# A chunked two-direction recurrence with stacked operands: products of 128 rows, transposes, and a new order of work

## What is computed

```python
def step(S, inp):
    rt, wt, kt, vt, at, bt = inp
    sa = jnp.einsum('bhvk,bhk->bhv', S, at)
    S = S * wt[:, :, None, :] + sa[..., None] * bt[:, :, None, :] + vt[..., None] * kt[:, :, None, :]
    return S, jnp.einsum('bhvk,bhk->bhv', S, rt)
...
s_fin, yd = wkv_scan(rh, decay, kd, vh, -kk, kk * a, S0[d], reverse=(d == 1))
```

## Time and profile before

| what | value |
|---|---|
| median of 3 runs | 2350.64 us (2346.11 to 2356.69) |
| the profiled execution's own time | 2349.85 us |
| its span | 2348.2 us |
| scan of layer 0, first product to last read | 415.1 to 621.3 us |
| scan of layer 1, window that holds it | 1617 to 1820 us |
| granted clock of PE, mean | 0.954 |

### The profile page before, as it was taken

How to read it: one execution, slowest core, us unless ns; L and a number is a source line. 1 busy time by engine, 2 the same in 40 slices (tenths; PEclk the granted TensorE clock), 3 DMA queues, 4 the chain that set the end, 5 groups by cost and what they waited for, 6 DMA issues and landing times. The chain is left out here.

```text
span 2348.2 us, 53901 instructions
## 1 busy us (share of the span) xinstructions
PE 2101.7 (90%) x23898; PEld 1349.7 (57%) x23898; DVE 720.6 (31%) x1768; ACT 487.9 (21%) x1120; POOL 274.7 (12%) x463
## 2 busy tenths in 40 slices
PE   6999899899899999999999789898999899987784
PEld 2454443889644444446556465554898788754442
DVE  1033334777431011310100032546676311200002
ACT  2123312333220000301111132323332301110011
POOL 0000000443100001101111100001343000011111
PEclk8999999899999999999999989998899999998996
DMA  7148716000121212448999821110000344799993
GB/s 287 61 154 344 305 65 226 3 4 4 56 90 54 108 54 108 181 161 328 398 383 395 306 90 51 69 50 1 4 4 4 146 159 188 274 378 397 395 406 122
DMA packets 55828, 399.91 MB, mean 170 GB/s; under 512 B 6672, under 2 KB 22928, under 8 KB 33648
## 3 DMA queue, kind: packets, MB, share of 16 engines
q1 hardware_dynamic: 43440, 361.94, 39.9%
q0 software_dynamic: 8576, 23.08, 2.6%
q10 hardware_dynamic: 3648, 12.45, 1.7%
HBM read 365.47 MB, written 31.98 MB: 169 GB/s over the span
## 5 line engine op out<-in xcount | busy, mean ns | idle before, releaser
L494 PE MATMUL ps<-H,memory 128*128 128x512 f32 (+2 forms) x1728 | 615.1, 512 | 11.6 <-DMA memory<-in_w_in 9.7
L494 PEld LDWEIGHTS ps<-H,memory 128*128 128x128 f32 (+1 forms) x1728 | 327.5, 190 | 286.5 <-issue 251.6
L731 PE MATMUL ps<-memory 64*64 64x32 f32 (+2 forms) x10112 | 329.0, 229 | 33.6 <-DVE memory L1624 10.1
L994 PE MATMUL ps<-memory 128*32 128x256 f32 x5120 | 298.8, 395 | 49.2 <-DMA memory<-in_eu 47.7
L731 PEld LDWEIGHTS ps<-memory 64*64 64x64 f32 x10112 | 316.4, 142 | 43.3 <-issue 21.3
L494 PE MATMUL ps<-memory 128*128 128x512 f32 (+3 forms) x928 | 319.2, 495 | 6.2 <-issue 3.0
L994 PEld LDWEIGHTS ps<-memory 128*32 128x32 f32 x5120 | 184.8, 114 | 160.0 <-issue 71.0
L494 PEld LDWEIGHTS ps<-memory 128*128 128x128 f32 (+1 forms) x928 | 173.8, 188 | 143.6 <-issue 127.3
L1019 PE MATMUL ps<-memory 128*32 128x256 f32 x2560 | 144.8, 380 | 5.0 <-ACT memory L1342 3.8
L1914 POOL TENSOR_TENSOR memory<-memory,cons 128x256 f32<-128x256 f32 x160 | 117.9, 752 | 122.5 <-DVE memory L1596 78.7
L1019 PEld LDWEIGHTS ps<-memory 128*32 128x32 f32 x2560 | 79.6, 110 | 59.9 <-ACT memory L1342 10.1
(11 more groups left out here) (251 smaller groups left out, 1804.9 us busy)
## 6 DMA issues: line engine op xcount, KB each, us to landing
memory<-in_eg SPq DMA_DIRECT2D x32, 2048.0 KB, 17.2
memory<-in_eu SPq DMA_DIRECT2D x32, 2048.0 KB, 23.0
memory<-in_ed SPq DMA_DIRECT2D x32, 2048.0 KB, 23.4
memory<-in_w_ada SPq DMA_DIRECT2D x24, 2048.0 KB, 9.5
memory<-in_w_in SPq DMA_DIRECT2D x20, 2048.0 KB, 7.6
expert_rows<-memory SPq DMA_DIRECT2D x4, 3456.0 KB, 23.7
memory<-in_w_out SPq DMA_DIRECT2D x4, 2048.0 KB, 7.8
memory<-expert_rows ACTq DMA_DIRECT2D x19, 384.0 KB, 10.4
```

What stands on the lines that cost most here:

```text
L494: ins = mm(ps[0:M, bank, 0:w], lhs(k), rhs(k), start=(k == 0), stop=(k == n - 1))
L731: ins = mm(out[cols, j], lhs[rows, j, :], rhs[rows, j], start=(n == 0), stop=(n == len(terms) - 1))
L994: ins = mm(out_.rearrange("p (x n) -> p x n", x=2), XGT[:, k, g * GROUP:g * GROUP + GROUP], sets[b][:, 0:2, k * 512 + c * P:k * 512 + c * ...
```

## The change

- The two heads' halves are kept in tiles with j outermost, so that one weight load takes 128 columns: `bE2` and `bKk` lie side by side in `BB`. `grams` is one product of 64 rows and 128 weight columns for each head, and the two heads write to different banks (`bank`).
- U and the values of a head lie one above the other in `UV` (64 + 64 partitions); so do the masked grams (`GR`) and the turned keys (`BK`). The last two terms of `readout` and both terms of `update` become one product of 128 rows and 64 weight columns.
- `turns` and `values` use PE's transpose, one record each, of 64 rows by 128 columns, in place of products with `eye`. `pick` on ACT gathers the two directions' chunks of V.
- `correct` is split: `correct_values` behind `couple`, then `grams` of both directions, then `correct_state`, then `solve`. Nothing stands between `correct_state` and `solve`, nor between `solve` and the first join.
- `turns` of both directions stand at level 1, `readout` of both at level 2, `update` of both at level 3, all behind `join(n,0)`; levels 0 and 4 have none; `values` stands behind level 4.
- ACT takes over: the unit diagonals of `XT` (`diagonals`; DVE then writes only the pairs, by `copy_predicated`), the state's decay (`decayed_state`, four ACTIVATEs for each direction), and the first visit of each output column (`first_read`, a copy; the memset of Y on POOL goes). Signs move into `B` and the masks.

```diff
+BK = [[pairs(piece(2)) for d in range(2)] for p in range(2)]
+GR = [[pairs(piece(2)) for d in range(2)] for p in range(2)]
+UV = [pairs(piece(2)) for d in range(2)]
+BB = [pairs(piece(2)) for d in range(2)]
+GAK = pairs(piece(2))
+VC = pairs(piece(2))
 TWICE = {"XT": [[quads(inv[d][:, 512 * p:512 * p + 256]) for d in range(2)] for p in range(2)],
...
+        "L": [quads(piece(1, (3,))) for d in range(2)],
+        "bE2": [BB[d][:, :, d] for d in range(2)],
+        "bKk": [BB[d][:, :, 1 - d] for d in range(2)]}
...
+    for j, d, h in problems:
+        ins = mm(part(d, 2, p)[side(h ^ d), j], BB[d][side(h), j, d], ER[p][d][side(h), 0, j],
+                 start=True, stop=True)
...
+def values(k):
+    pe.wait_ge(sem("values_moved"), picked(l * STEPS + k))
+    for d in both:
+        pe.wait_ge(sem("joined_copied"), level(l * STEPS + k, len(LEVELS) - 1, d))
+    for j in range(RJ):
+        for h in both:
+            ins = pe.transpose(ps[:, bank(h, 3), 256 + CH * j:256 + CH * j + CH], VC[side(h), j], eye[side(h), :])
+    ins.then_inc(sem("values"), 1)
...
 def grams(k, d):
...
+    if k:
+        pe.wait_ge(sem("state"), states(l, k - 1, d))
     if k >= 2 and streams(l, k - 2):
         pe.wait_ge(sem("read"), 2 * readouts(l, k - 2) - 1 + d)
     if streams(l, k):
         pe.wait_ge(sem("queries"), 2 * readouts(l, k) - 1 + d)
...
+    for j in range(RJ):
+        for h in both:
+            ins = mm(ps[:, bank(d, h), 128 * j:128 * j + CH * wide], BB[d][side(h), j], ER[p][d][side(h), 0:wide, j],
+                     start=True, stop=True)
+    ins.then_inc(sem("grams"), 1)
...
 def turns(k, d):
     pe.wait_ge(sem("masked"), nth(l * STEPS + k, d))
...
+    for j in range(RJ):
+        for h in both:
+            ins = pe.transpose(ps[:, bank(d, h), CH * j:CH * j + CH], BB[d][side(h), j], eye[side(h), :])
+    ins.then_inc(sem("turns"), 1)
...
+def correct_values(k):
...
+    for d in both:
+        pe.wait_ge(sem("masked"), nth(N, d))
+        pe.wait_ge(sem("values_moved"), held(N, d))
+    for j, d, h in problems:
+        ins = mm(part(d, 3, 0)[side(h ^ d), j], GAK[side(1 - d), j, h], UV[d][side(1 - d), j, h],
+                 start=(j == 0), stop=False)
+    ins.then_inc(sem("values"), 1)
...
+def correct_state(k):
     N, p = l * STEPS + k, k % 2
+    pe.wait_ge(sem("values"), corrected(N))
     for d in both:
         pe.wait_ge(sem("state"), states(l, k, d))
...
+    for j, d, h in problems:
+        ins = mm(part(d, 3, 0)[side(h ^ d), j], ER[p][d][side(h), 0, j], ONCE["S"][d][side(h), j],
+                 start=False, stop=(j == RJ - 1))
+        if j == RJ - 1 and h:
+            ins.then_inc(sem("rhs"), 1)
...
 def solve(k):
     N, p = l * STEPS + k, k % 2
     for d in both:
         pe.wait_ge(sem("rhs_copied"), nth(N, d))
         pe.wait_ge(sem("inverse"), inverses(N, 5, d))
...
+    for j, d, h in problems:
+        ins = mm(part(h ^ d, 3, 1)[side(d), j], TWICE["XT"][p][d][side(h ^ d), j], ONCE["RHS"][d][side(h ^ d), j],
+                 start=True, stop=True)
+        if j == RJ - 1 and h:
+            ins.then_inc(sem("u"), 1)
...
+def readout(k):
     N, p = l * STEPS + k, k % 2
...
+    for d in both:
+        pe.wait_ge(sem("u_copied"), nth(N, d))
+        if k + 1 < STEPS:
+            pe.wait_ge(sem("masked"), nth(N + 1, d))
+        if k + 2 < STEPS:
+            pe.wait_ge(sem("turned"), carried(l, k + 1, d))
+    for j, d, h in problems:
+        mm(part(d, 1, 0)[side(h), j], ONCE["S"][d][side(h), j], ER[p][d][side(h), 1, j], start=(j == 0), stop=False)
+    for j, d, h in problems:
+        ins = mm(part(d, 1, 0)[side(h), j], UV[d][:, j, h], GR[p][d][:, j, h], start=False, stop=(j == RJ - 1))
+        if j == RJ - 1 and h:
+            ins.then_inc(sem("readout"), 1)
...
+def update(k):
...
+    for j, d, h in problems:
+        ins = mm(part(d, 0, 0)[side(h), j], BK[p][d][:, j, h], UV[d][:, j, h], start=True, stop=True)
+        if j == RJ - 1 and h:
+            ins.then_inc(sem("step"), 1)
...
 for k in range(STEPS):
     more = k + 1 < STEPS
     couple(k)
     if k:
-        correct(k - 1)
+        correct_values(k - 1)
     grams(k, 0)
+    grams(k, 1)
     if k:
+        correct_state(k - 1)
         solve(k - 1)
-    grams(k, 1)
     for n in range(len(LEVELS)):
         join(k, n, 0)
-        if n == 0 and more:
-            turns(k, 0)
-        if k and n in (1, 2) and streams(l, k - 1):
-            readout(k - 1, n - 1)
-        if k and n == 3:
-            update(k - 1, 0)
-        if n == 4 and more:
-            values(k + 1, 0)
+        if n == 1 and more:
+            for d in both:
+                turns(k, d)
+        if n == 2 and k and streams(l, k - 1):
+            readout(k - 1)
+        if n == 3 and k:
+            update(k - 1)
         join(k, n, 1)
-        if n == 0 and more:
-            turns(k, 1)
-        if k and n == 3:
-            update(k - 1, 1)
-        if n == 4 and more:
-            values(k + 1, 1)
         grow(k, n, 0)
         grow(k, n, 1)
-correct(STEPS - 1)
+    values(k)
+correct_values(STEPS - 1)
+correct_state(STEPS - 1)
 solve(STEPS - 1)
...
+quarters = lambda rows, banks, x: ps[rows, banks, 256 * x:256 * x + 256].rearrange("p b (j n) -> p b j n", n=CH)
 def turns(k, d):
     act.wait_ge(sem("turns"), carried(l, k, d))
-    act.copy(BK[k % 2][d], ps[:, 4 * d, :]).then_inc(sem("turned"), 1)
+    act.copy(by_head(BK[k % 2][d]), quarters(slice(0, P), slice(bank(d, 0), bank(d, 1) + 1), 0)).then_inc(sem("turned"), 1)
...
+def pick(k):
...
+        act.wait_ge(sem("values"), turned(l * STEPS + k - 1))
...
+    act.copy(VC, v[:, :, other:None if after < 0 else after:c - other]).then_inc(sem("values_moved"), 1)
...
 def values(k):
+    act.wait_ge(sem("values"), turned(l * STEPS + k))
...
+        rows = side(1 - d)
+        act.copy(by_head(UV[d])[rows], quarters(rows, slice(bank(0, 3), bank(1, 3) + 1), 1)).then_inc(sem("values_moved"), 1)
...
-        act.activation(flat(ONCE["RHS"][d]), part(d, 3, 0), ACT.Copy, scale=-1.0).then_inc(sem("rhs_copied"), 1)
+        act.copy(flat(ONCE["RHS"][d]), part(d, 3, 0)).then_inc(sem("rhs_copied"), 1)
...
 def solve(k):
     for d in range(2):
         act.wait_ge(sem("u"), nth(l * STEPS + k, d))
-        act.copy(flat(ONCE["U"][d]), part(d, 3, 1)).then_inc(sem("u_copied"), 1)
+        rows = side(d)
+        act.copy(by_head(UV[d])[rows], quarters(rows, slice(bank(0, 3), bank(1, 3) + 1), 1)[:, ::-1 if d else 1]).then_inc(sem("u_copied"), 1)
...
+def diagonals(k):
+    for d in range(2):
+        act.copy(TWICE["XT"][k % 2][d], over_pairs(con_("eye")))
...
+def first_read(k, d):
+    act.wait_ge(sem("readout"), 2 * readouts(l, k) - 1 + d)
+    act.copy(Y[:, :, columns(k, d)], part(d, 1, 0).rearrange("p (j n) -> p j n", n=CH)).then_inc(sem("read"), 1)
+def decayed_state(k, d):
+    act.wait_ge(sem("state_added"), carried(l, k, d))
+    for j in range(RJ):
+        x = ONCE["S"][d][:, j]
+        ins = act.activation(x, x, ACT.Identity, scale=total[:, k % 3, d, j:j + 1])
+    ins.then_inc(sem("state"), 1)
...
-values(0)
...
         log_decays(k + 1)
     if k:
         solve(k - 1)
+        if more:
+            diagonals(k + 1)
     for n in range(len(LEVELS)):
         for d in range(2):
             act.wait_ge(sem("joined"), level(l * STEPS + k, n, d))
             act.copy(under(PS[n][d], n, d), under(part(d, 3, 0).rearrange("p (j n) -> p j n", n=CH), n, d))\
                .then_inc(sem("joined_copied"), 1)
-            if n == 0 and more:
+        if more and n == 1:
+            for d in range(2):
                 turns(k, d)
-        if more and n in (1, 2):
-            decays(k + 1, n - 1)
         if more and n < 2:
             decays_before(k + 1, n)
             growths(k + 1, n)
-    if more:
-        values(k + 1)
+        if more and n == 2:
+            for d in range(2):
+                decays(k + 1, d)
+        if n == 2:
+            pick(k)
+        if n == 3 and k and first(k - 1) and streams(l, k - 1):
+            for d in range(2):
+                first_read(k - 1, d)
+    if k:
+        for d in range(2):
+            decayed_state(k - 1, d)
+    values(k)
 correct(STEPS - 1)
...
+    tt(ONCE["MT"][d], half(d, 2, p), over_pairs(con_(f"strict{d}")), ALU.mult).then_inc(sem("coupling"), 1)
     turned = TWICE["XT"][p][d]
-    link(tt(turned, half(d, 2, p), over_pairs(con_(f"pair{1 - d}")), ALU.mult))
-    link(tt(turned, turned, over_pairs(con_("eye")), ALU.add))
+    dve.wait_ge(sem("exps"), grown(N, d))
+    link(dve.copy_predicated(turned, over_pairs(con_(f"pair{1 - d}")).bitcast(mybir.dt.uint32), half(d, 2, p)))
     dve.transpose(flat(ONCE["X"][d]), flat(turned)).then_inc(sem("inverse"), 1)
 def masks(k, d):
...
+    made = ps[:, bank(d, 0):bank(d, 1) + 1, :].rearrange("p h (j x n) -> p h j x n", x=2, n=CH)
+    over_heads = lambda mask: mask.unsqueeze(1).unsqueeze(1).broadcast_to([mask.shape[0], 2, RJ, CH])
     if streams(l, k):
```

(24 more changed lines are left out.)

136 lines of the change are left out of this document (54 added, 82 removed).

## The result

The changed kernel takes 2453.09 us (median of 4 runs, 2445.85 to 2464.94), the kernel before beside it on the same chip 2351.33: a ratio of 1.0438, 95% interval [1.0389, 1.0486]. The prediction said 2360 and at most 2385. The sign of the likeliest case was right, the size was not. The profiled execution, 2445.85 us at a mean granted clock of 0.901, is the fastest of the four; the others had 0.883 to 0.888.

A forecast was written before the change was run, and what follows sets the result against it. The prediction took PE as the bound, through the records it must issue and the clock it is granted. It summed 2349.85 - 33.8 (full-clock saving) + 44 (half clock) = 2360 us, range 2322 to 2385.

The forecast's parts named there:

- the likeliest case: Whole kernel: slower, at 2360 us; this forecast had chance 0.42 with its own range 2345 to 2378, slower in all 0.43.
- Levels 0 to 3: A full step's first four levels, with fewer records between joins: 12.6 us after the change for 15.5 before, at full clock.
- The head: Level 4 to the next level 0: 9.7 us for 9.8, savings in grams and values going into three opened waits.
- the second rival: ACT's scalings of the state do not overlap: 17 us more, 2377 us; decides from 0.2 us a scaling; chance 0.18.
- The clock term: Scan: clock falls around level 1 in nearly every step, returning with readout or update; 116 us of half clock, costing 44.
- The upper bound of the range: Clock in the scan: 150 us of half clock, costing 57 us, if it lasts a level longer.
- the full-clock sum: All steps of both layers without clock loss: 33.8 us less than before.
- The scan's ends: Last steps and the shorter last readout save 2.2 us each, 4.4; layer 0's first step saves 0.
- Clock stays up: Rival: the scan's clock stays mostly as before, half clock costing only 13 us; 2329 us, faster; chance 0.27.
- both half: Rival: the clock costs 22 us and unexplained PE stops remain, 7 us; 2345 us, no measurable change; chance 0.13.
- ACT's queue: Rival: ACT's state scalings ahead of correct_values do not overlap, +1.1 us a step, 17 us; 2377, slower; chance 0.18.

The follow-up runs named there:

- h5: Changed kernel with the head's old order and DVE scaling the state behind the last level's adds, no extra products; 2360 us, ratio 1.0029.
- e2: Changed kernel with the state's decay scaling back on DVE instead of eight ACT activations a step; 2423 us, ratio 1.027.
- e3: Changed kernel with the head's old order back: correct_values, correct_state, grams of direction 0, solve, grams of direction 1; 2379 us, ratio 1.0076.
- g2: Changed kernel with the block of both grams moved behind correct_state, ahead of solve; 2402 us, ratio 1.0213.
- g3: As f2, but both grams in one block behind correct_state, so the wait before the first join stays open; 2391 us, ratio 1.0171.
- h4: As f2, but DVE scales the state behind the last level's adds instead of ahead of them; 2353 us, ratio 0.9997.
- f2: Changed kernel with the head's old order, scaling on DVE, and 96 unused products in each step without readout; 2357 us, ratio 1.0025.
- f3: Kernel before the change, with grams of both directions in one block ahead of correct and solve; 2377 us, ratio 1.0107.
- f1: Changed kernel with the head's old order back and the state's scaling on DVE, no extra products; 2372 us, ratio 1.0096.
- h1: As f2, but the state's scaling of direction 0 on DVE and of direction 1 on ACT; 2377 us, ratio 1.0082.
- e1_fill: Changed kernel with unused products put into the three waits of each step's head; 2445 us, ratio 1.037.

## Why the prediction was wrong

**Levels 0 to 3: right.** 2.2, 3.1, 4.1, 3.2 us were worked out, 12.6 in all; at full clock h5 shows 2.41, 2.98, 4.15 and 3.28, 12.8. The stacked products run at the pace of two tiles, as assumed (readout's and update's records start 0.030 us apart).

**The head: 1.5 us short a step.** 9.7 us were worked out. The step from 471.12 (first join copy of level 4) to 482.29 (next of level 0), at full clock but for its end, took 11.2. From couple's start to correct_values are 2.08 us where the sum has 1.3: PE waits 1.6 us behind couple's last start and not 0.8, since a scaling is not 0.13 us but 0.25 (8 in 2.02). The 0.13 had no row behind it: it came from the lengths of plain copies, with an overlap that no row showed. That was the second rival's condition (from 0.2 on), and e2, 30 us less, shows that it mattered. The Trainium skill's ScalarE: Activation LUTs, What ACT_TABLE_LOAD costs, which the sum didn't use, gives 186 ns and 0.833 ns a column for an ACTIVATE, 93 ns more for each per-partition scale or bias, and 93 ns of overlap in a row. I estimate 0.33 us alone and 0.24 in a row from it for 64 columns, and the trace agrees (336 ns, and 0.25 in a row). The rest is small: correct_values 0.63 us for 0.5, correct_state to solve 1.63 for 1.45, solve to the first join 2.05 for 1.85, and 2.80 us outside for 2.65. 15 steps at 1.5 us are 22 us, so the full-clock sum is about -12 us, not -33.8.

**The clock term: the step that failed.** 116 us of half clock in the whole scan at 0.38 were put in, 44 us. The profiled execution has 311 us in the same places: 114 in the eight full steps (52 in the sum), 108 in the four later steps without readout (30), 50 in the two first steps (20) and 38 in the two last (14). Two things were read wrongly. The clock was taken to fall once a step, at level 1 with its transposes. It fell already in level 0, behind the open waits, and in most steps a second time in the head; e3, in which those transposes stay, ran its joins at full clock in layer 0 (L875 at 68.4 us, as in h5). And it was taken to return with update where no readout stands. It didn't: the first four steps of layer 1 ran at half clock for 118 of 123 us, the fifth for 20 of 28. The upper bound of the range, 150 us of half clock, had no row behind it.

**The sum again.** 311 us at h5's 0.34 are 106 us, and -12 + 106 = 94 for the 96 us between the two profiled executions' own times (2349.85 and 2445.85). At the 0.38 of the earlier trace rows it would be 106, so that it closes to 2 us is partly luck. The scan's ends are in these terms. In layer 1, where correct_values, correct_state, solve and the readouts follow with bare waits, it is 9.9 us from the last join copy (1811.24) to the first product behind the scan (1821.13) before, and 15.8 (1896.58 to 1912.39), at a clock of 0.68, after; the sum had 2.2 us saved there.

**The rivals.** "Clock stays up" and "both half" are out. ACT's queue was half of a true account. The sum priced the waits that the new order opens, but no rival gave the loss to the order, and it is the larger part: e3 gives back 74 of the 102 us. Order and scaling each open waits, and in a step with thin levels (few records between the joins) a wait is paid twice, once in idle and once in clock; e3, g2 and g3 show this. How much of e3's 74 us is wait and how much clock is settled only for layer 0's six steps: 34 us, of which 11 are idle (23.5 to 12.4) and 23 PE's busy time with the same records (153.3 to 130.6), so clock, 13.8 of it in the joins.

What stays open: why one execution of h4 or f2 keeps its clock and another loses it, and what in the stacked levels, beside the waits ahead of them, lets it fall.

## What to carry to other kernels

Before taking records out of a tight recurrence, look at what else they did: here grams, one direction ahead of solve and one ahead of the joins, covered two waits, and with turns, readout and update as many small products the clock stayed at 0.98 even with the waits open (f3), where the stacked form fell to 0.77. A saving at full clock (3.3 us a step here) is real only if the granted clock stays; find the place after the change where the longest idle meets the thinnest work, and price it with a row at half clock. When a late operation is on the chain, try moving it behind what others wait for (h5, 12 us below f1) before moving or splitting it between engines (e2, h1).

## What the runs showed of the chip

- The clock stayed down for over 100 us with PE busy at 99% (h5, first four steps of layer 1: 115.94 us at 0.51, PE busy 114.36), over half of its records being joins and grows of 32 columns. With 96 products of 64 columns added to each of these steps it stood at 0.91 in f2's profile, with the same added to h5 at 0.62 in h4's.
- Transposes of about the same length gained no time where products did (2373 and 2357, f1 2372); their clock lay between the two.
- Around runs of short records on four tiles PE stops without a releaser in the profile: 13 us in six steps of e1_fill, as the 0.81 in the earlier trace rows. The cause is not shown.
